# Experts' rows gathered as halves from two tables, up rows by slot and summed in four column groups of the array

## What is computed

```python
def peer(h, w_query, sub_keys1, sub_keys2, expert_down, expert_up):
    # h: tokens x 1024; expert_down, expert_up: 16384 x 1024, fp32
    qd = (xb @ w_query).reshape(-1, 8, 2, 128)
    s1 = einsum('thd,hkd->thk', qd[:, :, 0], sub_keys1)      # 8 heads, 128 keys each
    s2 = einsum('thd,hkd->thk', qd[:, :, 1], sub_keys2)
    v1, i1 = top_k(s1, 16); v2, i2 = top_k(s2, 16)
    cand = v1[..., :, None] + v2[..., None, :]               # 256 a head
    top_s, pos = top_k(cand, 16)
    idx = take_along_axis(cand_idx, pos)                     # 8 heads x 16 = 128 experts a token
    g = softmax(top_s)
    act = gelu(einsum('thkd,td->thk', expert_down[idx], xb))
    return einsum('thk,thkd->td', g * act, expert_up[idx])
```

## Time and profile before

| | |
|---|---|
| runs | 4389.1, 4391.28 and 4394.91 us, median 4391.28 |
| the profiled execution | span 4384.4 us from the first to the last instruction; with the median taken as its own time, 6.9 us lie around the span |
| busy over the span | TensorE 3487.9 us (80%), VectorE 2354.8 (54%), ScalarE 1050.6 (24%), GpSimd 1348.0 (31%) |
| expert phase | from the first gather at 1435.3 us to the end |
| gathers | 1024 of 1 MB (L1738), and 8 for the samples |
| DMA | 1269.3 MB, of which 1114.7 through GpSimd's queue |

### The profile page before, as it was taken

One profiled execution on the slowest core, in us unless ns is written; L12 is line 12 of the kernel. 1 busy time (PEld: TensorE's weight loads), 2 busy tenths in 40 slices (PEclk: granted clock), 3 DMA queues, 4 the chain that ended last, 5 costly groups with the idle time before them and its releaser, 6 DMA issues.

```text
span 4384.4 us, 39661 instructions
## 1 busy us (share of the span) xinstructions
PE 3487.9 (80%) x11633; PEld 1922.7 (44%) x11633; DVE 2354.8 (54%) x4730; ACT 1050.6 (24%) x3019; POOL 1348.0 (31%) x1232
## 2 busy tenths in 40 slices
PE   7699996469997687786787788778769778877876
PEld 1698774135555342352353344335325324324432
DVE  0651111746663767457546646646755755664574
ACT  1110112123341222222222222222222222222222
POOL 0020110400000343344444443434444444443442
PEclk9799997689998898898899889889889889988988
DMA  7232210642323899999999999999999999999996
GB/s 273 69 103 110 82 61 31 246 165 86 101 72 134 345 374 374 381 384 366 361 389 368 376 375 379 366 370 380 382 384 378 381 374 383 377 375 375 395 382 272
DMA packets 210634, 1269.30 MB, mean 290 GB/s; under 512 B 25875, under 2 KB 51099, under 8 KB 74060
## 3 DMA queue, kind: packets, MB, share of 16 engines
q0 software_dynamic: 159504, 1114.68, 64.3%
q1 hardware_dynamic: 50902, 152.03, 9.9%
HBM read 1218.26 MB, written 48.36 MB: 289 GB/s over the span
## 4 chain that ended last, share of the span: by engine, by line
DMA 26%; PE 25%; issue 8%; ACT 4%; POOL 3%; DVE 3%; POOLq 0%; ACTq 0%; DVEq 0%; SPq 0%
DMA e_buf<-in_experts,e_idx 26%; PE ps L1771 22%; PE ps L1502 3%; POOL e_buf L1738 3%; DVE e_buf L1840 2%; ACT e_wts L1812 2%; ACT e_diag L1816 1%; ACT e_acts L1810 1%; DMA e_buf<-in_experts,e_idxT 0%; DMA r_wq<-in_w_query 0%; POOLq L58 0%; DVE r_work L1590 0%; DVE r_row L1591 0%; DVE r_work L1587 0%; DVE r_pos L1550 0%
## 5 line engine op out<-in xcount | busy, mean ns | idle before, releaser
L1771 PE MATMUL ps<-e_buf,e_diag 128*128 128x512 f32 x4096 | 2026.0, 652 | 638.7 <-ACT e_diag L1816 635.2
L1840 DVE SCALAR_TENSOR_TENSOR e_buf<-e_buf,e_h 128x1024 f32<-128x1024 f32 x1024 | 1248.2, 1227 | 1091.6 <-DMA e_buf<-in_experts,e_idx 1075.2
L1738 POOL DMA_INDIRECT e_buf<-in_experts,e_idx x1024 | 1195.4, 1167 | 1605.1 <-PE ps L1771 1406.3
L1771 PEld LDWEIGHTS ps<-e_buf,e_diag 128*128 128x128 f32 x4096 | 836.0, 210 | 1758.4 <-issue 990.9
L1810 ACT ACTIVATE e_acts<-e_dots 128x4 f32<-128x4 f32 x256 | 52.6, 205 | 2085.0 <-DVE e_buf L1840 2076.4
L1816 ACT ACTIVATE e_diag<-ident,e_wts 128x128 f32<-128x128 f32 x1024 | 327.3, 390 | 27.8 <-ACT e_wts L1812 2.7
L1502 PEld LDWEIGHTS ps<-r_h2T,r_wq 128*128 128x128 f32 x2304 | 269.3, 193 | 34.0 <-issue 34.0
L1502 PE MATMUL ps<-r_h2T,r_wq 128*128 128x128 f32 x2304 | 269.9, 276 | 3.1 <-DMA r_wq<-in_w_query 3.1
L830 PE MATMUL ps<-xo_w_out,xo_catT 128*128 128x512 f32 x512 | 224.5, 592 | 1.7 <-DVE xo_x L863 1.7
L1812 ACT ACTIVATE e_wts<-e_acts,e_gate 128x1 f32<-128x1 f32 x1024 | 218.5, 284 | 9.2 <-ACT e_acts L1810 1.1
L74 PE MATMUL ps<-p_wth,hT_high 128*128 128x512 f32 (+1 forms) x432 | 170.6, 395 | 10.9 <-PEq L413 10.9
(11 more groups left out here) (338 smaller groups left out, 3007.2 us busy)
## 6 DMA issues: line engine op xcount, KB each, us to landing
w_mod_sb<-in_w_mod SPq DMA_DIRECT2D x12, 2048.0 KB, 8.4
e_buf<-in_experts,e_idx POOLq DMA_INDIRECT x1024, 9.1
p_wt<-in_w_rows SPq DMA_DIRECT2D x6, 2048.0 KB
proj_d<-p_ev POOLq DMA_DIRECT2D x48, 256.0 KB, 2.3
x_zgv<-proj_d SPq DMA_DIRECT2D x8, 1536.0 KB
p_w<-in_w_chan SPq DMA_DIRECT2D x20, 512.0 KB, 4.3
r_wq<-in_w_query SPq DMA_DIRECT2D x4, 2048.0 KB, 20.2
xbc_d<-p_res POOLq DMA_DIRECT2D x12, 516.0 KB, 3.0
```

Source lines behind the costliest of these rows:

```text
L1738: return pool.indirect_dma_start(out=buf[s][:], out_offset=None, in_=io["experts"], in_offset=bass.IndirectOffsetOnAxis(ap=numbers, axis=0 ...
L1771: last = nc.tensor.matmul(g.bank(cols), diag[:, k % RING, :], buf[k % RING][:, D + cols * 512:D + (cols + 1) * 512], start=(k == 0), stop= ...
L1840: V.scalar_tensor_tensor(out=down, in0=down, scalar=1.0, in1=row, op0=ALU.mult, op1=ALU.mult, accum_out=out).then_inc(sem, 1)
```

## The change

The tables stay apart, `down` and `up`, and so do the rings: `down[k % 8]` and `up[k % 8]`, each 128 x 1024. A gather brings 128 rows of 4 KB.

- **Down rows** are gathered as before, the token on the partition. A down buffer is free after its dot (`dotted`), not after a matmul.
- **Up rows are gathered by slot**: one gather brings the 128 up rows of one token, the slot on the partition. The indices of the whole tile are transposed for it (`turn_numbers`, TensorE, copied by ScalarE and by GpSimd in two parts). Token t = j * 32 + q is taken as the j-th of group q.
- **The sum** over the slots is then one over the partitions. The weights of the tile (`wts`, one product over 128 x 128 on VectorE) are transposed and placed by ScalarE into `cols`, one column at a distance of 32 among zeros (`place_columns`). A window of 32 columns over `cols` has token q's weights in its column q and zeros beside them. TensorE multiplies it with the up rows and adds into 32 partitions of banks 0 and 1, from j * 32 on: four tokens of a group use four column groups of the array. There are no diagonals and no weights slot by slot.
- **Stages.** The ups of tile n - 1 are gathered and summed in the stage in which the downs of tile n are gathered and dotted. Stage 0 has downs only. After stage 7 the ups of tile 7 are left; the samples' 8 downs go ahead of them and their 8 ups among them, and their sums after a quarter of the groups. `Finish` of tile n - 2 lies at the start of stage n.
- **h2** is kept in PSUM (banks 2 and 3), copied there by ScalarE, and `dot` reads it there. Gelu is done on 64 slots at a time.
- The router's transposes go to banks 4 and 5, `qT` has two buffers of four units instead of 16 units, the pieces of TensorE and ScalarE come one group later, SyncE's transfers are in another order, and `sel8` is now made in mix_sample by GpSimd instead of in modulation.

```diff
 # modulation / mix_sample
-                         (g.sel8, 1.0), (g.eye8, 1.0), (g.eps, EPS)):
+                         (g.eye8, 1.0), (g.eps, EPS)):
...
+            nc.gpsimd.memset(pick[:], 1.0).then_inc(picked, 1)
+            pool.wait_ge(picked, 1)
+            nc.gpsimd.affine_select(out=pick[:], in_=pick[:], compare_op=ALU.is_equal, fill=0.0, base=0,
+                                    pattern=[[-1, NS], [0, P]], channel_multiplier=1).then_inc(picked, 1)
...
-PE_PIECES = {q: 1 for q in range(1, 14)}
-ACT_PIECES = {q: 1 for q in (2, 4, 6, 7, 9, 10, 12, 13, 14, 18, 26)}
+PE_PIECES = {q: 1 for q in range(2, 15)}
+ACT_PIECES = {q: 1 for q in (3, 5, 7, 8, 10, 11, 13, 14, 15, 18, 26)}
...
-        buf = [sb(f"buf{s}", [P, 2 * D]) for s in range(RING)]
+        down, up = [sb(f"down{s}", [P, D]) for s in range(RING)], [sb(f"up{s}", [P, D]) for s in range(RING)]
...
         @block.gpsimd
+            nc.gpsimd.memset(cols[:], 0.0).then_inc(cleared, 1)
+
+            def gather_down(n, k, first):
+                if k in (0, HALF_SLOTS - RING):
...
+                    wait_apart(pool, rt.numbered, n * 2 + half + 1)
+                    nc.gpsimd.tensor_copy(idx[:, ks], rt.idx[:, ks]).then_inc(idx_kept, 1)
+                    wait_apart(pool, idx_kept, n * 2 + half + 1)
+                if not first or k >= RING:
+                    wait_apart(pool, dotted, n * SLOTS + k + 1 - RING)
+                gather(down[k % RING][:], "down", idx[:, k:k + 1], down_in[k % RING])
+
+            def gather_up(m, k):
+                if k == 0:
+                    wait_apart(pool, idxT_kept, m + 1)
+                if k % GROUP == 0:
+                    wait_apart(pool, summed, m * NG + k // GROUP + 1)
+                if k in (0, RING - GROUP):
...
+                    nc.gpsimd.tensor_copy(part(idxT), part(idxT_next)).then_inc(idxT_ready, 1)
...
+                t = (k % GROUP) * WIN + k // GROUP
+                gather(up[k % RING][:], "up", idxT[:, t:t + 1], up_in[k % RING])
+
+            def stage(n, first):
                 for k in range(SLOTS):
...
+                    gather_down(n, k, first)
+                    if not first:
+                        gather_up(n - 1, k)
...
         @block.tensor
+            def sums(m, q):
+                for j in range(GROUP):
+                    k = q * GROUP + j
+                    pe.wait_ge(up_in[k % RING], m * PER + 16 * (k // RING) + 16)
+                for half in range(2):
+                    for j in range(GROUP):
+                        k = q * GROUP + j
+                        at = WIN - 1 + k * WIN - q
+                        last = mm(g.ps[j * WIN:(j + 1) * WIN, half * 512:(half + 1) * 512], cols[:, at:at + WIN],
+                                  up[k % RING][:, half * 512:(half + 1) * 512], start=(q == 0), stop=(q == NG - 1))
+                last.then_inc(summed, 1)
+
+                    if turn_at == 0:
+                        if q == 0:
+                            turn_weights(n - 1)
+                            pe.wait_ge(cols_ready, n)
+                            pe.wait_ge(fin.sum_read, n - 1)
+                        sums(n - 1, q)
...
         @block.scalar
+            def keep_h2(n):
+                act.wait_ge(rt.h2_in, n * 16 + 16)
+                A(h2_ps, rt.h2[:], ACT.Copy).then_inc(h2_kept, 1)
...
+                if not first:
+                    gelu(n - 1, 1)
+                keep_h2(n)
+                if not first:
+                    place_columns(n - 1)
...
         @block.vector
+                if not first:
+                    weigh(n - 1)
                 dve.wait_ge(h2_kept, n + 1)
                 for k in range(SLOTS):
...
-                    dot(k % RING, h2[:], dots[:, k:k + 1], dotted)
+                    dve.wait_ge(down_in[k % RING], n * PER + 16 * (k // RING) + 16)
+                    dot(k % RING, h2_ps, dots[:, k:k + 1], dotted)
...
+                        if q == 0 and finish:
+
+                            dve.wait_ge(summed, (n - 1) * NG + RING // GROUP)
+                            fin.add(dve, n - 2, P)
...
-        "experts": np.concatenate([f["expert_down"][0], f["expert_up"][0]], axis=1),
+        "down": f["expert_down"][0], "up": f["expert_up"][0],
```

More of the change, by code:

```diff
@@ L1677, in experts @@
     NG = SLOTS // GROUP
+    WIN = P // GROUP
     with ExitStack() as st:
@@ L1753, in _, with gather @@
-            with pool.Fori(0, NT) as n:
-                tile(n)
-            pool.wait_ge(idxT_ready, 1)
-            for b in range(NS):
-                wait_apart(pool, summed, NT * SLOTS + b + 1)
-                gather(b % RING, idxT[:, b:b + 1]).then_inc(landed[b % RING], 16)
+            def gather(out, table, numbers, landed):
+                pool.indirect_dma_start(out=out, out_offset=None, in_=io[table],
+                                        in_offset=bass.IndirectOffsetOnAxis(ap=numbers, axis=0)).then_inc(landed, 16)
@@ L1781, in _ @@
+            stage(0, FIRST_TURN)
+            route = rt.tensor(pe, 2)
+            for q in range(NG):
+                if q == 0:
+                    turn_numbers(1)
+                    turn_weights(0)
+                    pe.wait_ge(cols_ready, 1)
+                sums(0, q)
+                if q == 1:
+                    pe.wait_ge(idxT_kept, 2)
+                drive(route, PE_PIECES.get(q, 0))
+            with pe.Fori(2, NT) as n:
+                stage(n, 0)
             pe.wait_ge(rt.gated, 2 * (NT + 1))
-            for m, src in enumerate((rt.num, rt.gate)):
-                last = nc.tensor.transpose(g.bank(2, cols=NS, at=m * NS), src[0:NS, :], g.ident[0:NS, 0:NS])
+            for i, src in enumerate((rt.num, rt.gate)):
+                last = tr(g.bank(6, cols=NS, at=i * NS), src[0:NS, :], g.ident[0:NS, 0:NS])
@@ L1784, in _ @@
             last.then_inc(turn_ps, 1)
[L1785 to L1792 removed]
+            turn_weights(NT - 1)
@@ new lines, in _ @@
+            pe.wait_ge(cols_ready, NT)
+            pe.wait_ge(fin.sum_read, NT - 1)
+            for q in range(NG):
+                sums(NT - 1, q)
+                if q == NG // 4:
+                    for b in range(NS):
+                        pe.wait_ge(s_weighed, b + 1)
+                        pe.wait_ge(s_up_in[b], 16)
+                        for half in range(2):
+                            last = mm(g.bank(4 + half, rows=NS), wpad[:, b, :],
+                                      s_up(b)[:, half * 512:(half + 1) * 512], start=(b == 0), stop=(b == NS - 1))
+                    last.then_inc(s_summed, 1)
@@ L1859, in tile @@
-                    if k == GROUP - 1 and not first:
-                        dve.wait_ge(summed, n * SLOTS + RING)
-                        fin.add(dve, n - 1, P)
-                    if k == 2 * GROUP - 1 and not first:
-                        fin.scale(dve, n - 1, P)
-            tile(0, True)
-            with dve.Fori(1, NT) as n:
-                tile(n, False)
+                            drive(own, FIRST_DVE_PIECES.get(q, 0))
+                        drive(route, DVE_PIECES.get(q, 0))
```

304 lines of the change are left out of this document (176 added, 128 removed).

## The result

The changed kernel takes **4282.7 us** (median of 4 runs, 4280.6 to 4285.5) against 4392.0 us for the kernel before beside it on the chip: a ratio of 0.9745, 95% interval 0.9731 to 0.9758. The forecast was 4340 us with a range from 4290; the time lies 57 us under the forecast and 7 us under the range. The sign was right. The profiled execution has a span of 4282.4 us and took 4283.9.

What follows compares the result with a forecast made beforehand. Bound: the ring's round trip over a nearly full DMA. Stage 0 ends at 1684, seven stages of 348 reach 4120, the tail's 194 gives 4314, 19 more 4333; with 6.9 from span to median, 4340 us, range 4290 to 4470.

Steps and rivals of the forecast that it cites:

- 144 gathers of the tail: Tail after stage 7: 128 ups of tile 7, 8 sample downs and 8 ups at 1.35 us each, 194 us.
- after the last gather: End of the kernel: 4.2 landing, 3.4 matmuls, 8.1 to the store's issue, 3.3 to the end: 19 us.
- What bounds the kernel now: Expert phase of the kernel before, 362.0 us a tile: the ring's round trip over a nearly full DMA, no engine's work.
- Stage 0: First stage, with downs only: VectorE-bound by 128 dots and routing, 234 us plus 3% for waits, 241 us, ending at 1684.
- S = 348: Time of each of the seven stages with both rings: GpSimd's sum of 345 us plus 3 for the tile's start.
- one real wait per group of four: GpSimd in a stage: release takes 0.77 us against 0.30, so 32 x 0.47 = 15 us.
- the 3 us for the tile's start: Added per stage because the first sum waits until VectorE has done four dots and read the previous total.
- floor: DMA's least time for a stage: 330 us of 4 KB-row gathers plus 3.8 for h2, x1 and y, 334 us.
- PSUM operand against held-up GpSimd: Forecast: dots reading h2 from PSUM don't hold gathers up, 1.246 us each. Rival: they do, S = 382, 4595 us; chance 0.05.
- Dry queue: Rival in the stages: one late sum or dot stops both rings; S from 353 to 365, 4375 to 4460 us; chance 0.25.
- Fixed cost per gather: Rival on DMA: halved gathers each cost extra, 3.0 us a slot, S = 388, total 4642 us; chance 0.07.
- Column groups in turn: Rival on TensorE: the four column groups don't overlap; tail slower, 4362 us, or 4417 at the low clock; chance 0.13.

Runs made afterwards that it cites:

- before_half: The kernel before with gathers of half the bytes, 4 KB rows from the down table alone; 3883.5 us, a tile 298.8 us.
- before_psum: The kernel before with h2 kept in PSUM, the router's transposes moved to banks 4 and 5; 4358.8 us, ratio 0.9925.
- wide_rows: The changed kernel with one gather of 128 rows of 8 KB for two slots: half the gathers, the same bytes; 4235.2 us.
- half_rows: The changed kernel gathering only the first 2 KB of each 4 KB row, same number of gathers, half the bytes; 4224.6 us.
- h2_sbuf: The changed kernel with h2 in SBUF, so its dots read two SBUF operands; 4490.6 us.
- one_group: The changed kernel with all four slots of a group summed in column group 0 of the array; 4710.6 us.

## Why the prediction was right in sign and wrong in size

From the forecast of the profiled span, 4333, to 4282.4:

| step | forecast | measured | difference |
|---|---|---|---|
| end of stage 0 | 1684 | 1679.3 | -5 |
| seven stages | 7 x 348 | 7 x 330.9 | -120 |
| wait for the samples' indices | none | 10.2 | +10 |
| 144 gathers of the tail | 194 | 13.5 + 240.7 | +60 |
| after the last gather | 19 | 22.3 | +3 |

*What bounds the kernel now*: right as far as shown. before_half shows that it isn't the bytes alone (half of them take 63 of 362 us off), before_psum that it isn't GpSimd. That it is "no engine's work" isn't shown: TensorE is busy 285 of the 362 us, and 88% in before_half.

*Stage 0*: right to a microsecond (241.3 us against 241), VectorE-bound, and for the reason given: from the first dot at 1443.9 to stage 1's first at 1686.3 VectorE is busy 233 us, where 234 were taken.

*S = 348, the step that failed.* Its first term was exact (256 gathers at 1.246; the held-up few add 4 us, where 5 were taken). What failed is "one real wait per group of four", 15 us, and the 3 us for the tile's start: 5 us are there in place of the 18. I took the 0.77 us from the earlier trace rows, where GpSimd runs ahead and waits for each release. In the changed kernel GpSimd is the late one and mostly finds its semaphores set; the waits of a queue that is ahead can't be added to the work of the queue that sets the time. The DMA's "floor" of 334 was too high as well: the changed kernel runs below it, and the same bytes in rows of 8 KB take 323 in wide_rows. It rests on the 0.159 us of a 4 KB row from two transfers beside the gathers; the whole mix moves at 419 GB/s in the stretch above. With the waits that are there the sum is 319 + 6 + 4 + 5 = 334, against 330.9 measured. In these 330.9 the samples' loads hold 9.5 us of one stage, a term that the forecast didn't have.

*The tail.* The mechanism was right (a turn of eight slots sets it), with two of its terms too small. Landing was taken as 4.2 us from the least landing of 1 MB; after four issues 1.25 us apart it is 6.5. That each transfer stands behind the ones before fits half_rows, where the median falls from 6.1 to 3.7 us, but no run shows it alone. The matmuls were taken as 1.7: that is the higher clock (1.92 measured), and I called it the most at the low one, counting eight passes where there are sixteen. In the tail's starved stretch the granted clock is 0.66 and most groups take 3.64. The turn is 14.7 and not 10.4, 1.84 a gather and not 1.30.

*The two errors had opposite signs*, -120 and +73, so that the total was nearer than its parts was luck.

*PSUM operand against held-up GpSimd*: right, h2_sbuf shows it. The rival's price, S = 382, was too high (360), because fewer gathers start where a dot holds them than in the kernel before: the mean is 1.085 us and not 1.167. The prediction's reading of the Trainium skill (SBUF — State Buffer, Who interferes with whom), by which the dots would hold nothing up, overlooks that a gather reads its row numbers from SBUF.

*Dry queue*: it didn't happen with eight down buffers; with four, S = 341.5. (Its price at S = 355 is 4340 + 7 x 7 = 4389, not 4391.) *Fixed cost per gather*: refuted, 4 KB rows ran at 419 GB/s, as fast as GpSimd issues them, where the earlier trace rows has 7.63 MB in 18 us, 424. (The Trainium skill, DMA: Bandwidth & Descriptors, Rules for kernel authors, wants 1 MiB for a DMA; gathers of 512 KB lost at most about 1% here, as long as the queue was full.) *Column groups in turn*: wrongly priced. I gave it 4362 to 4417, in the tail alone; one_group took 4710.6, since the longer groups stretch the stages too, from 330 to 378 us. I had called them hidden there.

## What to carry to other kernels

Find for each queue and engine what it needs alone, take the largest, and don't add to it the waits seen on an engine that ran ahead: here the engine that was late found most of its semaphores set. Cost a pipeline's drain as a separate stage with its own ring, with landing times of queued transfers and the clock of a starved TensorE, and look there for buffers that the finished stages left free: here eight of them were worth 67 us. Look for single large loads in the stages as well: 4 MB cost 9.5 us. When two resources are both near full, halve each alone; one run each tells which is in front and by how much.

## What the runs showed of the hardware that was not expected

- A gather of 128 rows is issued in 0.94 us with 0.30 between two, whether a row has 2, 4 or 8 KB (977 ns in half_rows' downs, 958 to 964, 945 in wide_rows): 1.25 us is GpSimd's price of a gather. With gathers of 0.25 MB it was the limit (328 us a stage, DMA at 73%), with 1 MB the queue was (323 us, 420 GB/s); that they meet at about 0.5 MB is an estimate from 1.25 us x 420 GB/s.
- A gather that starts within a VectorE product of two SBUF operands, 1.23 us long, ends no earlier than 0.8 us after that product; all 387 that started 0.06 to 0.95 us into a dot in h2_sbuf were held. One that is already under way isn't touched. With one operand in PSUM none of 685 was held.
- A float32 matmul shows as two passes; 16 passes over four column groups of 32 took 1.92 us at the higher clock and 3.64 at the lower one, about as much as four passes in a row.
